# Two gate tiles moved ahead of the first head pair, and the first pair's cached keys turned by VectorE

## The reference, cut to what matters

```python
h = rmsnorm(x, g_mix_pre)                       # 544 x 1024
proj = h @ w_in                                 # 1024 x 4608
q, k, v, xr, gb, gates = split(proj)            # 512 each, gates 2048
o_attn = block attention of q over k, v         # samples: also over 256 cached keys and values,
                                                # gathered through page_table (16 pages of 128)
xc = conv(xr); hseq = rglru(xc)                 # gated linear recurrence
o_rnn = hseq * gelu(gb)
gate_a, gate_r = split(gates)                   # 1024 each
merged = sigmoid(gate_a) * (o_attn @ w_pa) + sigmoid(gate_r) * (o_rnn @ w_pr)
x = x + rmsnorm(merged @ w_out, g_mix_post)
x = x + rmsnorm((silu(f @ w_g) * (f @ w_u)) @ w_down, g_ffn_post)   # f = rmsnorm(x, g_ffn_pre)
```

## Time and profile before

| what | value |
|---|---|
| median of 3 runs | 778.83 us |
| the profiled execution's own time | 781.89 us |
| its span in the trace | 779.8 us |
| TensorE (PE) busy | 766.1 us, 98% |
| weight loads (PEld) | 724.2 us, 93% |
| VectorE (DVE) busy | 482.4 us, 62% |
| ScalarE (ACT) busy | 357.2 us, 46% |
| GpSimd (POOL) busy | 70.4 us, 9% |
| granted clock of TensorE, mean | 0.997 of full |

### The profile page before, as it was taken

The page is one execution under the profiler, slowest core; times in us unless marked ns, Lnnn a source line. Parts: engine busy times, 40 slices in busy tenths (PEclk is TensorE's granted clock), DMA queues, the critical chain, the costliest instruction groups (busy, mean ns, idle before and its releaser), DMA issues.

```text
span 779.8 us, 16411 instructions
## 1 busy us (share of the span) xinstructions
PE 766.1 (98%) x5975; PEld 724.2 (93%) x5975; DVE 482.4 (62%) x756; ACT 357.2 (46%) x625; POOL 70.4 (9%) x156
## 2 busy tenths in 40 slices
PE   8999999999999999999999999999999999999996
PEld 6879999999899899997799999999999999999996
DVE  4655756847647634774567987887777777222323
ACT  5436534534625532334456555455555565222322
POOL 5521102102012010004000000000000010000000
PEclk9999999999999999999999999999999999999998
DMA  6745655555544224516552333233333125434333
GB/s 191 180 110 114 161 127 111 151 131 123 142 110 111 65 85 142 183 55 182 169 163 55 109 108 99 83 87 108 108 108 107 55 76 169 117 94 107 90 92 126
DMA packets 196979, 91.68 MB, mean 118 GB/s; under 512 B 65142, under 2 KB 190538, under 8 KB 196940
## 3 DMA queue, kind: packets, MB, share of 16 engines
q1 hardware_dynamic: 194270, 84.63, 40.0%
q0 software_dynamic: 2576, 6.45, 2.7%
q10 hardware_dynamic: 94, 0.09, 0.1%
HBM read 82.37 MB, written 6.81 MB: 114 GB/s over the span
## 4 chain that ended last, share of the span: by engine, by line
PE 94%; POOL 2%; DMA 1%; ACT 1%; issue 0%; DVE 0%; DVEq 0%; POOLq 0%; ACTq 0%
PE ps L958 32%; PE ps L1312 27%; PE ps L1377 17%; PE ps L1211 6%; PE ps L1281 3%; PE ps L1070 1%; PE ps L1084 1%; PE ps L1102 1%; PE ps L987 1%; DMA bias_rev<-dist_shift 1%; PE ps L1144 1%; PE ps L1055 1%; PE ps L1219 1%; PE ps L1115 1%; PE ps L990 0%
## 5 line engine op out<-in xcount | busy, mean ns | idle before, releaser
L1923 DVE TENSOR_TENSOR w_lo<-w_raw,w_hi 128x1024 fp32r<-128x1024 f32 (+1 forms) x67 | 80.1, 1197 | 131.7 <-ACT w_hi L1450 131.4
L958 PE MATMUL ps<-xin_hi,w_hi 128*128 128x272 f32 x576 | 125.4, 297 | 2.1 <-DVE w_lo L1923 1.0
L1450 ACT ACTIVATE w_hi<-w_raw 128x1024 fp32r<-128x1024 f32 (+1 forms) x68 | 70.0, 1030 | 119.3 <-PE ps L1377 78.1
L958 PE MATMUL ps<-xin_hi,w_lo 128*128 128x272 f32 x576 | 120.4, 288 | 0.0
L958 PE MATMUL ps<-xin_lo,w_hi 128*128 128x272 f32 x576 | 120.2, 288 | 0.0
L958 PEld LDWEIGHTS ps<-xin_hi,w_hi 128*128 128x128 f32 x576 | 90.4, 189 | 10.9 <-issue 7.6
L958 PEld LDWEIGHTS ps<-xin_lo,w_hi 128*128 128x128 f32 x576 | 91.1, 189 | 0.0
L958 PEld LDWEIGHTS ps<-xin_hi,w_lo 128*128 128x128 f32 x576 | 90.6, 189 | 0.0
L1377 PE MATMUL ps<-hid_hi,w_hi 128*128 128x272 f32 (+2 forms) x352 | 75.4, 289 | 0.4 <-DVE hid_lo L2339 0.4
L1377 PE MATMUL ps<-hid_lo,w_hi 128*128 128x272 f32 (+2 forms) x352 | 74.9, 288 | 0.0
L1377 PE MATMUL ps<-hid_hi,w_lo 128*128 128x272 f32 (+2 forms) x352 | 74.9, 288 | 0.0
(11 more groups left out here) (337 smaller groups left out, 1748.8 us busy)
## 6 DMA issues: line engine op xcount, KB each, us to landing
w_raw<-in_w_in_dram SPq DMA_DIRECT2D x72, 256.0 KB, 3.5
g_raw<-in_w_gate_up_dram SPq DMA_DIRECT2D x40, 256.0 KB, 3.7
w_raw<-in_w_down_dram SPq DMA_DIRECT2D x40, 256.0 KB, 3.0
u_raw<-in_w_gate_up_dram SPq DMA_DIRECT2D x20, 256.0 KB, 3.1
e_raw<-in_w_gate_up_dram SPq DMA_DIRECT2D x20, 256.0 KB, 4.2
kc<-in_cache_k_dram SPq DMA_DIRECT2D x64, 64.0 KB
vc<-in_cache_v_dram SPq DMA_DIRECT2D x64, 64.0 KB
wo_raw<-in_w_out_dram SPq DMA_DIRECT2D x12, 256.0 KB, 4.1
```

The costliest lines, as they stand in the source:

```text
L958: mm = e.matmul(ps[:, bank + h, 0:HT], wt[:, kw, :], xt[:, kx, h * HT:h * HT + HT], start=first and wt is wh and xt is xh, stop=last and ( ...
L1450: e.activation((to or w_hi[s])[:, 0:k, :], w_raw[s][:, 0:k, :], ACT.Copy).then_inc(hi_done, count)
L1923: e.tensor_tensor(wl[:, 0:k, :], w_raw[s][:, 0:k, :], wh[:, 0:k, :].bitcast(F32), ALU.subtract).then_inc(lo_done, count)
```

## The change

Two of the four gate tiles behind the last pair are put ahead of pair 0 (`GT_HEAD`), as tiles 0 and 1; all later numbers and counts move by two tiles or one use of a slot. The transposes of the tokens now stand between the parts of gate tile 0 instead of tile 0 of the pair. Pair 0 becomes like the others: `load_keys_0`, `cache_T` and `cache_copy` are gone, its keys are loaded in blocks and turned by VectorE. In SP's queue tiles 2 and 3 (q and k of pair 0) are loaded between groups of pages; tile 4 (v of pair 0) comes in `iteration(0)` at `j == 2`, behind `biasT` and `bd_all`. `KC_PAGES_0` is gone: the next pair's keys now begin at `j == 4`. The loops over the tail's tiles are written out on SP and ScalarE. `bd_all` lies two gate tiles further on.

```diff
-C_TAIL = PAIRS * TILES_IT
-GT_TAIL = 2 * KD - PAIRS * GT_IT
+GT_HEAD = 2
+C_TAIL = GT_HEAD + PAIRS * TILES_IT
+GT_TAIL = 2 * KD - PAIRS * GT_IT - GT_HEAD
...
-KC_PAGES_0 = (), (), (), (), (), range(0, 4), range(4, 9), range(9, 14)
...
             for i in range(2):
-                load(i, i, wi[:, :, 512 * i:512 * i + P])
+                load(i, i, wi[:, :, 2560 + (PAIRS * GT_IT + i) * P:2560 + (PAIRS * GT_IT + i + 1) * P])
...
-            def load_keys_0():
-
-                for j in range(DEC_B * NPG):
-                    e.dma_start(kc[:, j, :], page_of(cache_k, 0, j).rearrange("o t c -> t (o c)")).then_inc(kc_in, 16)
...
             def iteration(it, first=False, last=False):
                 for j in range(TILES_IT):
-                    if first and j < 4:
+                    if first and j < 2:
                         pass
                     elif j < 5:
-                        load(it * TILES_IT + j, j % 2, wi[:, :, bass.ds(it * P + 512 * j, P)])
+                        load(it * TILES_IT + (GT_HEAD + j), j % 2, wi[:, :, bass.ds(it * P + 512 * j, P)])
...
-                    pages = (KC_PAGES_0 if first else KC_PAGES)[j]
+                    pages = KC_PAGES[j]
...
-            load_keys_0()
-            load(2, 0, wi[:, :, 2 * 512:2 * 512 + P])
-            load(3, 1, wi[:, :, 3 * 512:3 * 512 + P])
+            load_keys(0, range(0, 4))
+            load(GT_HEAD, 0, wi[:, :, 0:P])
+            load_keys(0, range(4, 10))
+            load(GT_HEAD + 1, 1, wi[:, :, 512:512 + P])
+            load_keys(0, range(10, DEC_B * NPG))
             iteration(0, first=True)
...
-                if first:
-                    e.wait_ge(sp_act, 2)
-                    begin(0); part(0, 0, 5, hs=(0,)); x_T(3); part(0, 5, 7, hs=(0,)); x_T(4); part(0, 7, 8, hs=(0,))
-                    e.wait_ge(xt_lo, 9)
-                    part(0, 0, 8, hs=(1,))
-                    e.wait_ge(small_c, 2)
-                    begin(1); part(1, 0, 5); cache_T(0); part(1, 5, 8)
-                    cache_T(1); begin(2); part(2, 0, 2); cache_T(2); part(2, 2, 4); cache_T(3); part(2, 4, 7)
-                    scores_s(); part(2, 7, 8)
-                else:
-                    begin(0); part(0, 0, 8)
-                    begin(1); part(1, 0, 8)
-                    begin(2); part(2, 0, 5); scores_s(); part(2, 5, 8)
+                begin(0); part(0, 0, 8)
+                begin(1); part(1, 0, 8)
+                begin(2); part(2, 0, 5); scores_s(); part(2, 5, 8)
...
+            e.wait_ge(sp_act, 2)
+            gate_part(0, 0, 0, 0, 5, hs=(0,)); x_T(3)
+            gate_part(0, 0, 0, 5, 7, hs=(0,)); x_T(4)
+            gate_part(0, 0, 0, 7, KD, hs=(0,))
+            e.wait_ge(xt_lo, 9)
+            gate_part(0, 0, 0, 0, KD, hs=(1,))
+            e.wait_ge(small_c, 2)
+            gate_part(1, 0, 1, 0, KD)
+
+            heads(0)
...
             for i in range(GT_TAIL):
-                s = i % 2
-                split_ready(C_TAIL + i)
-                e.wait_ge(tile_free[s], 4 * PAIRS + i // 2 + 1)
-                steps(s, 2 * s, xin_hi, xin_lo, [(k, k) for k in range(KD)], True, True).then_inc(tile_done, 1)
-                if i == 1:
+                gate_part(C_TAIL + i, (C_TAIL + i) // 2, i % 2, 0, KD)
+                if i == 0:
                     e.wait_ge(st_saved, PAIRS)
...
(ScalarE)
                 next_hi(0)
                 if first:
-                    e.wait_ge(sp_dve, SP_ABS)
-                    e.activation(sp[2][:, :], sp[1][:, :], ACT.Exp, scale=-1.0).then_inc(sp_act, 1)
-                    cache_copy(0)
+                    gate_out(1, 1, PAIRS * GT_IT + 1)
 
                 next_hi(1)
                 done(0)
                 e.activation(halves(qT[:, :]), two(0), ACT.Copy, scale=DH ** -0.5).then_inc(tile_free[0], 1)
-                if first:
-                    cache_copy(2)
                 next_hi(2)
                 exp_s()
...
+            hi(1, 0, 1)
+            e.wait_ge(sp_dve, SP_ABS)
+            e.activation(sp[2][:, :], sp[1][:, :], ACT.Exp, scale=-1.0).then_inc(sp_act, 1)
+            hi(2, 1, 0)
+            gate_out(0, 0, PAIRS * GT_IT)
...
(VectorE)
-                if first:
-                    next_lo(0)
-                    parameters()
-                    next_lo(1); cache_copy(1)
-                    k_copy(); cache_copy(3)
-                    next_lo(2)
-                else:
-                    next_lo(0)
-                    keys_turn(0); keys_turn(1)
-                    next_lo(1)
-                    keys_turn(2); keys_turn(3)
-                    k_copy()
-                    next_lo(2)
+                next_lo(0)
+                keys_turn(0); keys_turn(1)
+                next_lo(1)
+                keys_turn(2); keys_turn(3)
+                k_copy()
+                next_lo(2)
...
+            lo(1, 1)
+            parameters()
+            lo(2, 0)
+
             heads(0, first=True)
```

More of the change, by code:

```diff
@@ L197, in program @@
     st_out = put("st_out", [36, DR], where=[lgt_at])
-    bd_all = put("bd_all", [P, 2, PAIRS, RGB], where=[gates_at + 4 * PAIRS * GT_IT * T])
+    bd_all = put("bd_all", [P, 2, PAIRS, RGB], where=[gates_at + 4 * (PAIRS * GT_IT + GT_HEAD) * T])
     prT = put("prT", [P, 2, PT_W, P], where=[kcT_at])
@@ L641, in iteration @@
                 for j in range(TILES_IT):
-                    if first and j < 4:
+                    if first and j < 2:
                         pass
                     elif j < 5:
-                        load(it * TILES_IT + j, j % 2, wi[:, :, bass.ds(it * P + 512 * j, P)])
+                        load(it * TILES_IT + (GT_HEAD + j), j % 2, wi[:, :, bass.ds(it * P + 512 * j, P)])
                     else:
-                        load(it * TILES_IT + j, j % 2, wi[:, :, bass.ds(it * (GT_IT * P) + 2560 + (j - 5) * P, P)])
+                        load(it * TILES_IT + (GT_HEAD + j), j % 2, wi[:, :, bass.ds(it * (GT_IT * P) + 2560 + (j - 5) * P, P)])
                     if j == 1:
@@ L690, in _ @@
             store_kv(PAIRS - 1)
-            with e.Fori(0, GT_TAIL // 2) as n:
-                for s in range(2):
-                    load(n * 2 + (C_TAIL + s), s, wi[:, :, bass.ds(n * (2 * P) + 2560 + (PAIRS * GT_IT + s) * P, P)])
+            for i in range(GT_TAIL):
+                g = PAIRS * GT_IT + GT_HEAD + i
+                load(C_TAIL + i, i % 2, wi[:, :, 2560 + g * P:2560 + (g + 1) * P])
             def load_out(k):
@@ L1034, in mi_wait @@
                     e.wait_ge(mi_free, it * 5 + (use + 1))
-                def cache_T(f):
-                    if f == 0:
-                        e.wait_ge(kc_in, 256)
-                    else:
[L1041 to L1044, removed]
                 def scores_s():
@@ L1167, in heads, with gate_part @@
                 begin(7); values(); part(7, 0, 8)
-            heads(0, first=True)
+            def gate_part(i, uses, s, k0, k1, hs=(0, 1)):
+                if k0 == 0 and 0 in hs:
+                    split_ready(i)
+                    e.wait_ge(tile_free[s], uses + 1)
+                mm = steps(s, 2 * s, xin_hi, xin_lo, [(k, k) for k in range(k0, k1)], k0 == 0, k1 == KD, hs=hs)
+                if k1 == KD and 1 in hs:
+                    mm.then_inc(tile_done, 1)
+            e.wait_ge(sp_act, 2)
[7 more added lines that the diff above has]
+            heads(0)
             with e.Fori(1, PAIRS) as it:
@@ L1597, in heads, with gate_out @@
                 e.activation(ocat_hi[:, bass.ds(it + PAIRS, 1), :], dd[:, 0:T], ACT.Copy).then_inc(orn_hi, 1)
+            def gate_out(i, s, g):
+                e.wait_ge(tile_done, i + 3)
+                e.activation(halves(gates[:, g, :]), two(s), ACT.Tanh, scale=0.5).then_inc(tile_free[s], 1)
+            hi(1, 0, 1)
[3 more added lines that the diff above has]
+            gate_out(0, 0, PAIRS * GT_IT)
             heads(0, first=True)
@@ L1601, in _ @@
                 heads(it)
-            with e.Fori(0, GT_TAIL // 2) as n:
-                for s in range(2):
-                    i = n * 2 + (C_TAIL + s)
-                    hi(i + 1, n + (C_TAIL + s + 1) // 2, 1 - s)
-                    e.wait_ge(tile_done, i + 3)
-                    dst = gates[:, :, :].rearrange("p k t -> p (k t)")[:, bass.ds(n * (2 * T) + (PAIRS * GT_IT + s) * T, T)]
-                    e.activation(halves(dst), two(s), ACT.Tanh, scale=0.5).then_inc(tile_free[s], 1)
+            for i in range(GT_TAIL):
+                hi(C_TAIL + i + 1, (C_TAIL + i + 1) // 2, 1 - i % 2)
+                gate_out(C_TAIL + i, i % 2, PAIRS * GT_IT + GT_HEAD + i)
             def out_hi(k):
```

41 lines of the change are left out of this document (17 added, 24 removed).

## The result

The kernel after took **787.35 us** (median of 4 runs, 786.86 to 788.24), the kernel before beside it 778.84 (778.17 to 779.4): ratio **1.0094**, interval 1.0068 to 1.0121. (The medians alone would give 1.0109.) That is slower, as forecast, but by more than three times the forecast amount. The median lies above the top of the range (786.5); by the ratio the time is 1.0094 x 778.83 = 786.2, just inside it. The profiled execution took 786.86 us; its span is 785.0, 5.2 longer than the 779.8 of before.

What follows compares the result with a forecast made beforehand. PE, busy 98% of the span, was taken as the bound; waits of 5.6 + 1.5 + 0.1 less a saving of 4.9 gave +2.3 us on 778.83, so 781.1, with a range of 776.5 to 786.5.

Steps and rivals of the forecast that it cites:

- the mechanism: SP's queue in pair 0: pages in blocks delay v's weights, so PE stands still 5.6 us for v's `w_lo`.
- The saving of 4.9: Pair 0 up to `scores(3)`: 4.9 us saved from 16 key transposes (1.4), two waits (2.7) and gaps (0.8).
- The tail costs nothing: After pair 3: the mix stage would begin with 8.6 us in hand, so two tiles less cover cost nothing.
- both instants stay: Head of the kernel: PE still begins tile 0 at 19.70 and tile 1 at 28.12 with gate tiles there.
- the 3.1 us taken off in the sum: Last step: the profiled execution is 3.1 us above the median, so 784.2 became 781.1 on the runs' scale.
- the queue between v and tile 7: SP's loads behind v in pair 0: PE waits 1.5 us for tile 5's weights and 0.1 at `probs_T(2)`.
- the dearer case: SP's group of four pages at 49.63 in the earlier trace: 6.42 us, 1.6 a page; 1.22 was taken instead.
- my sum between tile 5 and tile 7: SP's queue: tile 6 issued at 54.8, 6.7 for values, then 4.9 plus 0.3 for keys; tile 7 at 66.7.
- The queue keeps up: Rival, SP's queue ahead of pair 0: at 0.6 us a page no wait is left, 773.9; chance 0.20.
- The rule that went with it: SP's queue: starting a DMA is usually short beside the DMA, so order hardly matters and 4.9 us is won (773.9).
- The clock falls: Rival, PE at v: the standstill drops the clock to half speed, 2.2 us more, 783.3; chance 0.12.
- The tail is bare: Rival, tail: with two tiles of cover PE waits for pair 3's recurrence, 782.5; chance 0.03.

Runs made afterwards that it cites:

- run 8: Kernel before with pair 0's 16 pages loaded in blocks and turned by VectorE, no gate tiles at the head: 793.19 us, ratio 1.0173.
- run 6: Kernel after with pair 0's pages in their own layout, turned by TensorE, gate tiles still at the head: 777.64 us, ratio 0.9975 against before.
- run 12: The kernel of run 6 with the next pair's keys begun at j = 5 again: 776.55 us, ratio 0.9972 against before.
- run 5: Kernel after, unchanged, measured once more on another chip: 787.34 us, ratio 1.0101 against before.
- run 3: Kernel after with the next pair's keys begun at j = 5 again in pair 0: 786.62 us, ratio 1.0085 against before.
- run 4: Kernel after with 50 unused identity transposes between k and v of pair 0 to keep PE busy: 791.24 us, ratio 1.0134 against before.
- run 9: Kernel after with the edits of run 3 and run 4 together: 788.73 us, ratio 1.01 against before.
- run 7: Kernel after with value loads interleaved between pages, v's weights before the last two pages, values and next keys later: 785.21 us, ratio 1.0082 against before.
- run 10: The queue order of run 7 without interleaving, all 16 value loads ahead of the first page: 784.17 us, ratio 1.0053 against before.
- run 11: Kernel after with pair 0's keys loaded in blocks from fixed addresses, pages 0 to 15: 788.76 us, ratio 1.0104 against before.
- run 2: Kernel after with v's weights issued right behind k's, ahead of the last 6 pages: 789.58 us, ratio 1.0117 against before.

## Why the prediction was wrong in size

**Right.** The direction, and the mechanism: SP's issue of the pages in blocks makes v's weights late, and PE stands at v for `w_lo`, with ScalarE's rounding before it waiting for the DMA (run 8 shows the cost alone, run 6 its absence). The saving of 4.9 holds between the traces: with 1.4 of transposes kept, 3.5 should be left of it in run 6, and the spans of run 6 and of before differ by 3.6, of which 0.45 is an earlier start. In medians it is only 1.8 (run 12: 2.3). The two profiled executions of before are at the long end of its spans, and why the medians show less was not settled. The tail costs nothing.

**The step that failed first: "both instants stay", and the 3.1 us taken off in the sum.** The instants do not stay from one execution to the next, whatever the change, and the consequence is in the last step of the sum. PE's first tile begins at 16.9 to 18.0 in eight of the fourteen traces and at 19.2 to 19.7 in the other six, with the head tiles (runs 6 and 12) or without (run 8 and before); the profile of before was of the second kind and that of after of the first. SP's pages begin at 16.1 to 17.6 in every trace in which the value loads stand ahead of them. A kernel bound by PE gains the 2.4 us of an early start (runs 6 and 12). For the kernel after the reading is that it does not, since its weights come by SP's clock and PE only waits longer. Three things speak for it: its ten runs here and in run 5 have spans of 785.0 to 786.4, without the two groups of run 12; run 3, with a late start, has the shortest span of its five; and in run 3 the first tile began 2.15 later than in the kernel after, but v only 0.61 later (53.60), its waits at k and v being 1.7 shorter. No trace shows the kernel after itself with a late start, so this is argued and not shown. I took 3.1 us off to come from the profiled execution of before to the runs' median, and applied the same 3.1 to the kernel after. There nothing was to be taken off: its profiled execution is 0.5 *below* its median (0.9 above in run 5). 3.1 + 0.5 = 3.6 of the 6.25 us between 781.1 and 787.35 lie here. The start can account for about 2.4 of them; what makes up the rest stays open.

**The other 2.7: the queue between v and tile 7.** On its own scale the forecast was 784.2, measured 786.86. `probs_T(2)` was to begin at 76.0 and began at 78.73. By steps:

| step | predicted | measured |
|---|---|---|
| a page in blocks, the 16 of pair 0 | 1.22 | 1.36 |
| end of the keys | 39.5 | 42.5 |
| v's weights issued | 44.5 | 46.5 |
| v begins | 51.9 | 53.0 |
| tile 5's weights issued | 53.0 | 52.9 |
| `scores(3)` | 60.9 | 62.1 |
| tile 7's weights issued | 66.7 | 69.8 |
| `probs_T(2)` | 76.0 | 78.7 |

The early pages were 3.0 late (16 x 0.14 = 2.2 for the price, 0.8 for the two loads between them), but `biasT`, `bd_all` and the first values went faster than in the earlier trace rows, and tile 5 was on time at 52.9. What decided came behind it: tile 6's own load (1.8) was left out of my sum between tile 5 and tile 7, and 4 pages of the next pair's keys took 6.31 instead of 4.9. 1.8 + 1.4 = 3.2. The earlier trace rows had shown 6.42 for just this group, 4 pages beside the weights of pair 0; it was in the range as "the dearer case" and should have been the value of that term. Run 3 shows the term from its other side: with these pages gone from there, `probs_T(2)` has no wait.

**A wait not predicted.** PE waited 2.00 at k. My sum has no line for k; with its own prices it would be 16.41 + 10 x 1.22 + 1.77 = 30.4 for the issue of k's weights, and they went out at 32.95, since the six pages before them took 9.64 / 6 = 1.61 each. PE's early start is not the whole reason: run 3 waited 1.86 and run 4 2.26 at k with a late one. The wait adds nothing by itself, since v's wait behind it would be that much longer.

**The rivals.** *The queue keeps up* is refuted: at 1.36 a page it cannot. The rule that went with it, from the Trainium skill, "DMA: Bandwidth & Descriptors", section "Issuing engines are not separate DMA queues", says "usually", and this is a case where it does not hold: 0.57 against 1.36 us of issue a page is what parts run 6 from run 5 (beside which engine turns the keys, and 1.4 us of transposes that run 6 has more), ratio 0.9975 against 1.0101. *The clock falls* came true as a fact, 0.50 for v's first 3.2 us, but hardly as a price. PE lost 1.6 us in v and reached `scores(3)` at 62.13; `lgt_s`, which it needs, was written only by 61.86, so at most 0.3 was lost:

```profile
61.41 0.45 DVE L2050 CUSTOM_DVE_ANT_0 lgt_s<-ps,mask_s 128x288 f32<-128x288 f32 x1
```

Runs 4 and 9 kept the clock up over v and were not faster, but in both it fell at a later wait, so the price in this kernel rests on the row above. On the clock itself the trace agrees with the Trainium skill, "TensorE: Matmul & The Clock Gate", section "The HAM clock gate": down to half in a standstill, back after work. *The tail is bare* did not occur.

**Balance.** PE's waits 10.5, plus 1.6 of slow clock, less the waits and transposes saved (4.9) and less the early start (2.5) gives +4.7; the span shows +5.2. The 0.5 that is left was not traced.

## What to carry to other kernels

When a queue that issues loads is full, each microsecond of issue ahead of a load is a microsecond of its arrival, even while the DMA engines have room (busy for 0.32 here); ask what a layout costs in the *issuer's* time before it is chosen to spare another engine, and add up every load between two points, its own neighbours included. Moving one late load forward only moves the wait to the next load. Before a sum is carried from one profiled execution to the median, look whether the part that varies (here the start) still reaches the end in the changed kernel.

## What the runs showed of the hardware that was not expected

- Issue time on SP goes with the shape of a load more than with its bytes: 64 KB in 128 pieces of 512 bytes took 0.57 us, in 512 pieces of 128 bytes 1.31 to 1.39 (means of 16, with the address from a register or fixed), and 256 KB of weights 0.84.
- A value load on SP is not hidden between DMA issues: 0.63 us each between the pages (run 7 against run 10), 0.55 each ahead of them.
- The start comes in two kinds, 16.9 to 18.0 and 19.2 to 19.7; the spans of run 12's executions lie in two groups 2.4 us apart. In the late kind four opening matmuls take 3.78 us (row of the kernel before, below; in that of after 1.98). The early kind is not the one with the higher clock: from 9 to 11 us the granted clock was 0.50 in the trace of after and 1.00 in that of before. The cause was not tried.

```profile
5.78 3.78 PE L990 MATMUL ps<-g_one,ones 1*128 1x512 f32 x4
```
```profile
5.41 1.98 PE L987 MATMUL ps<-g_one,ones 1*128 1x512 f32 x4
```

- The granted clock fell to about half not only in the wait of 6.9 us but behind waits of 2.1 (run 11), 2.4 (run 10), 2.5 (run 4), 2.6 (run 9), 2.8 and 3.6 (run 2) and 3.0 us (run 7). It stayed at 1.00 behind the 1.6 us of the kernel after at the probabilities, and also behind the waits of 2.0 to 2.3 us at k (the kernel after, runs 2, 4, 5, 9 and 11). So the length of a standstill alone does not tell whether the clock falls. Where it does fall, the standstill costs more than its own length: in run 4, 1.5 us on top of 2.5.
